# Six norms of the first block of a two-block transformer taken by token tiles, with their gains as rows

## What is computed

```python
def rmsnorm(x, g):
    xf = x.astype(jnp.float32)
    y = xf * lax.rsqrt(jnp.mean(xf * xf, axis=-1, keepdims=True) + EPS)
    return (y * g.astype(jnp.float32)).astype(x.dtype)

def first_block(x, ...):
    for l in range(DEPTH):
        x = x + 0.5 * swiglu(rmsnorm(x, g_ffn1[l]), w_ffn1_gu[l], w_ffn1_down[l])
        x = x + hybrid_mixer(rmsnorm(x, g_mix[l]), w_in[l], ...)
        x = x + 0.5 * swiglu(rmsnorm(x, g_ffn2[l]), w_ffn2_gu[l], w_ffn2_down[l])
    return rmsnorm(x, g_final)

def hybrid_layer(x, c, ...):            # second block, twice
    mod = jax.nn.silu(c) @ w_ada + b_ada
    sh1, sc1, gt1, sh2, sc2, gt2 = jnp.split(mod, 6, axis=-1)
    h = adaln(rms_norm(x, g_mix), sh1, sc1)
    ...
    x = x + gt1[:, None, :] * (mixed @ w_out)
    h = adaln(rms_norm(x, g_mlp), sh2, sc2)
    u = jnp.square(jax.nn.relu(h @ w_up))
    x = x + gt2[:, None, :] * (u @ w_down)
```

## Time and profile before

| what | us |
|---|---|
| median of 3 runs | 2094.83 |
| lowest, highest | 2093.02, 2095.72 |
| span of the profiled execution | 2091.6 |
| TensorE busy | 1985.8 (95%) |
| DVE busy | 1556.4 (74%) |
| ACT busy | 1017.8 (49%) |
| POOL busy | 37.0 (2%) |

### The profile page before, as it was taken

One profiled execution on the slowest core, in us unless ns is written; L12 is line 12 of the kernel. 1 busy time (PEld: TensorE's weight loads), 2 busy tenths in 40 slices (PEclk: granted clock), 3 DMA queues, 4 the chain that ended last, 5 costly groups with the idle time before them and its releaser, 6 DMA issues.

```text
span 2091.6 us, 32432 instructions
## 1 busy us (share of the span) xinstructions
PE 1985.8 (95%) x11828; PEld 1737.4 (83%) x11828; DVE 1556.4 (74%) x2748; ACT 1017.8 (49%) x1550; POOL 37.0 (2%) x72
## 2 busy tenths in 40 slices
PE   6999999989999999999899999998899979999998
PEld 5888988878888888898888887898688868887887
DVE  7887467679877887556688887775766768677766
ACT  5445444644445445445555445466444445554443
POOL 0000000000000000000000000000000000000000
PEclk9999999999999999999999998999999989998999
DMA  7774443247774775443246763431355534233553
GB/s 293 279 284 183 161 152 122 91 171 273 278 254 146 287 283 213 157 162 122 91 168 248 280 246 123 179 147 59 133 181 184 194 138 180 93 125 113 190 189 133
DMA packets 76900, 382.05 MB, mean 183 GB/s; under 512 B 8960, under 2 KB 9088, under 8 KB 55552
## 3 DMA queue, kind: packets, MB, share of 16 engines
q1 hardware_dynamic: 67392, 329.78, 43.0%
q0 software_dynamic: 9408, 50.90, 7.0%
HBM read 379.60 MB, written 1.05 MB: 182 GB/s over the span
## 4 chain that ended last, share of the span: by engine, by line
PE 83%; DVE 10%; ACT 4%; issue 2%; DMA 1%; SPq 0%; DVEq 0%; ACTq 0%
PE psum L641 20%; PE psum L557 16%; PE psum L559 15%; PE psum L558 15%; PE psum L644 10%; DVE weights_low_a L1366 2%; ACT weights_high_a L1029 1%; PE psum L875 1%; DVE weights_low_b L1366 1%; PE psum L605 1%; DVE h_high_low L1415 1%; PE psum L877 1%; PE psum L850 1%; PE psum L876 1%; PE psum L788 1%
## 5 line engine op out<-in xcount | busy, mean ns | idle before, releaser
L641 PE MATMUL psum<-h_high_low,weights_high_a 128*128 128x512 f32 x1840 | 665.8, 403 | 7.4 <-DVE h_high_low L1411 4.6
L1366 DVE TENSOR_TENSOR weights_low_a<-raw_a,weights_high_a 128x2048 fp32r<-128x2048 f32 (+1 forms) x232 | 460.0, 1984 | 124.4 <-ACT weights_high_a L1029 121.8
L644 PE MATMUL psum<-h_high_low,weights_low_a 128*128 128x256 f32 x1840 | 518.5, 282 | 0.0
L1029 ACT ACTIVATE weights_high_a<-raw_a 128x2048 fp32r<-128x2048 f32 (+1 forms) x232 | 386.1, 1664 | 126.6 <-PE psum L559 122.8
L641 PEld LDWEIGHTS psum<-h_high_low,weights_high_a 128*128 128x128 f32 x1840 | 349.8, 190 | 100.4 <-DVE h_high_low L1415 6.4
L644 PEld LDWEIGHTS psum<-h_high_low,weights_low_a 128*128 128x128 f32 x1840 | 351.5, 191 | 7.0 <-issue 1.0
L1366 DVE TENSOR_TENSOR weights_low_b<-raw_b,weights_high_b 128x1024 fp32r<-128x1024 f32 x224 | 273.4, 1221 | 55.9 <-ACT weights_high_b L1029 55.1
L1029 ACT ACTIVATE weights_high_b<-raw_b 128x1024 fp32r<-128x1024 f32 x224 | 236.0, 1054 | 109.5 <-PE psum L559 109.4
L1080 ACT ACTIVATE up_low_products<-psum 128x512 f32<-128x512 f32 (+1 forms) x146 | 74.0, 507 | 407.1 <-PE psum L644 407.1
L557 PE MATMUL psum<-weights_high_b,gated_high 128*128 128x512 f32 x608 | 240.4, 395 | 1.0 <-DVE gated_low L1484 1.0
L558 PE MATMUL psum<-weights_low_b,gated_high 128*128 128x512 f32 x608 | 240.5, 396 | 0.0
(11 more groups left out here) (296 smaller groups left out, 3226.6 us busy)
## 6 DMA issues: line engine op xcount, KB each, us to landing
ada_weights<-in_w_ada POOLq DMA_DIRECT2D x64, 768.0 KB, 5.7
raw_a<-in_w_ffn_a_a SPq DMA_DIRECT2D x44, 1024.0 KB, 7.2
raw_a<-in_w_ffn_b_a SPq DMA_DIRECT2D x44, 1024.0 KB, 7.2
raw_a<-in_w_ffn_a SPq DMA_DIRECT2D x64, 512.0 KB, 4.5
raw_b<-in_w_ffn_b SPq DMA_DIRECT2D x64, 512.0 KB, 3.2
raw_a<-in_w_proj_a SPq DMA_DIRECT2D x28, 1024.0 KB, 5.5
raw_a<-in_w_gate_a SPq DMA_DIRECT2D x26, 1024.0 KB, 4.8
raw_b<-in_w_ffn_a_b SPq DMA_DIRECT2D x44, 512.0 KB, 3.5
```

Of the source, the lines that this page charges most:

```text
L641: pe.matmul(ps[:, bank, :], whi[0][:, p, c:c + P], hboth[:, k, :, :].rearrange("p a b -> p (a b)"), start=k == 0, stop=False, skip_group_c ...
L644: last_mm = pe.matmul(ps[:, bank, SEQ:2 * SEQ], wlo[0][:, p, c:c + P], hhi[:, k, :], start=False, stop=k == KD - 1, skip_group_check=True)
L1029: act.activation(whi[kind][:, p, 0:width], raw[kind][:, p, 0:width], ACT.Copy).then_inc(now().hi_ready[kind], 1)
L1366: dve.tensor_tensor(wlo[kind][:, p, 0:width], raw[kind][:, p, 0:width], whi[kind][:, p, 0:width].bitcast(F32), ALU.subtract).then_inc(lo_r ...
```

## The change

1. **The six norms of the first block (`row_norm`).** The gain comes as a row of 128x1024, loaded by POOL's queue (`load_gain`, 512 KB each, two buffers in turn), instead of as a column. DVE multiplies x by the row factor and by the gain at once, in two halves of 128x512 for each tile (L1544). TensorE transposes tile 0 (8 transposes into banks 2 and 3), works on it, then transposes tile 1 (banks 4 and 5). ACT writes h high in two copies of 128x4x128 for each tile, DVE h low in two subtractions of the same size (L1551). DVE does the last sum of x, (1,1), after the scale of tile 0, and the scale of tile 1 after the low part of tile 0. The squares of the second tile's second half stand behind high(0) on ACT.
2. **First step after a norm by token tiles.** `first_gate_up` does the first gate-up step as pieces of 128 tokens: 64 multiplies instead of 32 (L689, 2x128 columns, and L691, 128 columns). In a projection (`project_rows`) tile 0's first piece comes before `second_tile()`. The ada columns are cut in 9 before the first transposes and 15 after the second ones.
3. **Ada bank.** The ada columns of the first block go to bank 1 and no longer wait for `x_ready`; only those ahead of norm 7 keep bank 4 and the wait.
4. **Last downs.** The last two `down` steps of every feed-forward run as (j-1: 00, 01, 10), (j: 00, 01), (j-1: 11), (j: 10, 11).
5. **Tail of w_out.** Rows 0 to 4 are done in all pieces, then rows 5, 6 and 7 per piece (`OUT_TAIL = 5`), in the mixers of both blocks. The splits of the next b0 are taken out of the merge and put after the norm.
6. **Next layer's a0, a1.** In a feed-forward that closes a layer, ACT splits the next layer's a0 and a1 in its last two steps, and DVE makes the low part of a0 before the last gate chain.
7. **Small.** Block 1's PSUM banks for projections follow a list of 8; the final gain comes in the same two buffers; parameters of the first block are narrower by 24 columns.

```diff
+OUT_TAIL = 5
...
-ROW_BANKS = 6
+ROW_BANK = {1: (0, 6, 7, 2, 3, 4, 5, 1), 2: (0, 1, 2, 3, 4, 5)}
...
                     retire_last_layer(k, blk)
                 if blk == 1:
 
-                    pool.wait_ge(now().scale_ready, 2 * NT + 1)
+                    pool.wait_ge(now().scale_ready, 2 * NT)
+                    load_gain(3 * l + 1)
+                    load_gain(3 * l + 2)
+                    pool.wait_ge(now().scale_ready, 4 * NT + 1)
+                    load_gain(3 * l + 3)
                     ada_loads(l, 1)
...
+                def turn(t):
+                    for half in range(2):
+                        pe.wait_ge(now().scale_ready, 2 * NT * (n - 1) + 2 * t + half + 1)
+                        for i in range(KD // 2):
+                            k = half * (KD // 2) + i
+                            m = pe.transpose(ps[:, ROW_TURN_BANK + 2 * t + half, i * P:(i + 1) * P],
+                                             xn[:, t, k * P:(k + 1) * P], ident)
+                        m.then_inc(now().turned, 1)
+
+                def second():
+                    turn(1)
+                    if ada:
+                        ada[0](ADA_FIRST, ADA_COLUMNS)
+
+                if ada:
+                    ada[0](0, ADA_FIRST)
+                turn(0)
+                state["h_waited"] = 0
+                state["halves"] = True
+                state["second"] = second
+                state["ada_copied"] = ada[1] if ada else None
...
+                def first_gate_up():
+
+                    wait_ffn_part(l, blk, 0, n0, 0)
+                    early = 1 if state["ada_copied"] else gates
+
+                    def piece(m, t):
+                        for k in range(KD):
+                            need_h(k, t)
+                            c = (m * KD + k) * P
+                            out = ps[:, m, :].rearrange("p (a b) -> p a b", a=2)
+                            cols = slice(t * P, (t + 1) * P)
+                            pe.matmul(out[:, :, cols], whi[0][:, 0, c:c + P], hboth[:, k, :, cols],
+                                      start=k == 0, stop=False, skip_group_check=True)
+                            last_mm = pe.matmul(out[:, 1, cols], wlo[0][:, 0, c:c + P], hhi[:, k, cols],
+                                                start=False, stop=k == KD - 1, skip_group_check=True)
+                        return last_mm
+
+                    for m in range(early):
+                        piece(m, 0)
+                    second_tile()
+                    for m in range(early):
+                        last_mm = piece(m, 1)
+                    if early < gates:
+                        need_ada_bank()
+                        for t in range(NT):
+                            last_mm = piece(1, t)
+                    last_mm.then_inc(now().used[0], 1)
+
                 def gate_up(j, p):
-                    if isinstance(j, int) and j == 1:
-                        need_ada_bank()
+                    if isinstance(j, int) and j == 0 and state["halves"]:
+                        first_gate_up()
+                        return
                     wait_ffn_part(l, blk, 0, n0, j)
...
+                def last_downs():
+
+                    j, p = tiles - 1, (tiles - 1) % 2
+                    need_down(j - 1)
+                    for t, h in ((0, 0), (0, 1), (1, 0)):
+                        down_piece(1 - p, t, h, False, False)
+                    need_down(j)
+                    for h in range(2):
+                        down_piece(p, 0, h, False, True).then_inc(now().sums_ready, 1)
+                    down_piece(1 - p, 1, 1, False, False).then_inc(now().used[1], 1)
+                    down_piece(p, 1, 0, False, True).then_inc(now().sums_ready, 1)
+                    down_piece(p, 1, 1, False, True).then_inc(now().used[1], 1)
 
...
+                for t in range(NT):
+                    for h in range(2):
+                        for k in range(OUT_TAIL, KD):
+                            m = out_piece(k, t, h)
+                            if k == OUT_TAIL and (t, h) == (NT - 1, 1):
+                                m.then_inc(now().used[1], 1)
+                        if (t, h) != (NT - 1, 1):
+                            m.then_inc(now().sums_ready, 1)
+                m.then_inc(now().used[0], 1)
 
...
+                def high(t):
+                    for half in range(2):
+                        seen(now().turned, "turned")
+                        k = half * (KD // 2)
+                        act.activation(hhi[:, k:k + KD // 2, t * P:(t + 1) * P],
+                                       ps[:, ROW_TURN_BANK + 2 * t + half, :].rearrange("p (k c) -> p k c", c=P),
...
+                if first:
+                    split_high(0, 1, 0, 0)
+                high(0)
+                row_guess(1, first)
+                high(1)
+                if after:
+                    after()
+
...
+            def next_layer_high(n):
+
+                k = layer_at[0]
+                if k + 1 < 2 * LAYERS:
+                    enter_layer(k + 1)
+                    split_high((k + 1) % LAYERS, (k + 1) // LAYERS + 1, 0, n)
+                    enter_layer(k)
+
...
-                        split_high(l, blk, 1, n0 + j + 1)
+                        if not closing:
+                            split_high(l, blk, 1, n0 + j + 1)
+                        if n0 and j >= tiles - 2:
+                            next_layer_high(j + 2 - tiles)
...
+                def scale(t):
+                    row_factor(t)
+                    for half in range(2):
+                        c = slice(half * 512, (half + 1) * 512)
+                        dve.scalar_tensor_tensor(xn[:, t, c], x[:, t, c], rstd[:, t:t + 1], gain[:, c],
+                                                 ALU.mult, ALU.mult).then_inc(now().scale_ready, 1)
+
+                def low(t):
+                    for half in range(2):
+                        seen(now().hhi_ready, "hhi")
+                        k, cols = slice(half * (KD // 2), (half + 1) * (KD // 2)), slice(t * P, (t + 1) * P)
+                        dve.tensor_tensor(hlo[:, k, cols],
+                                          ps[:, ROW_TURN_BANK + 2 * t + half, :].rearrange("p (k c) -> p k c", c=P),
+                                          hhi[:, k, cols].bitcast(F32), ALU.subtract).then_inc(now().hlo_ready, 1)
+
+                if update:
+                    update(0, 0)
+                    update(0, 1)
+                    update(1, 0)
+                scale(0)
+                if update:
+                    update(1, 1)
+                if between:
+                    between()
+                low(0)
+                scale(1)
+                low(1)
+                if after:
+                    after()
...
+                        await_next_layer(dve, n0)
+                        next_layer_low(0)
...
-                        merge(l, 1, Walk(SLOTS1, FF1 + 16, 3, YT1, G_AT[1]), FF1 + 16, 3, False)
-                        norm(lambda k: g(16 + k), after=lambda: split_low(l, 1, 0, FF1 + 23))
-                        feed_forward(l, 1, FF1 + 22, FF1, 2)
+                        update = merge(l, 1, Walk(SLOTS1, FF1 + 16, 3, YT1, G_AT[1]), FF1 + 16, 3, False)
+                        row_norm(3 * l + 2, update=update,
+                                 after=lambda: (split_low(l, 1, 0, FF1 + 23), split_low(l, 1, 1, FF1 + 22)))
+                        pending_update = feed_forward(l, 1, FF1 + 22, FF1, 2)
```

338 lines of the change are left out of this document (195 added, 143 removed).

## The result

The changed kernel takes 2099.66 us in the median of 20 runs, the kernel before 2094.78 in 20 runs beside it: a ratio of 1.0026, with an interval of 1.0018 to 1.0035, so some 5 us slower. The forecast was +6.55 against the profiled span. The profiled execution of after has a span of 2099.3, 7.7 above that of before. Stretches at half clock don't fall on the same places in every execution.

What follows compares the result with a forecast made beforehand. TensorE, busy 95% of the span, was taken as the bound. Terms of 3.9 + 0.8 + 0.8 + 4.0 + 2.0 + 1.4 - 6.35 gave +6.55 on 2091.6, 2098.2, and 2101.3 as median; range 2089 to 2107.

Steps and rivals of the forecast that it cites:

- my 3.2 between span and median: Whole kernel: the median of the runs lies 3.2 us above the profiled span, added to 2098.2 to give 2101.3.
- The gain's load: Norm 1: 512 KB of gain rows on POOL's queue make the slots land later by 0 to 1.3 us, taken 0.6.
- The second turn: Norm 1: DVE scales tile 1 after low(0), so TensorE waits about 1.1 us at tile 1's transposes.
- The small multiplies: Norm 1: the first gate-up step by token tiles costs 2.2 us more, partly at half clock.
- the 2.05: Norms 3 and 6: tile 1's scale, turn, copy and low part hold TensorE for 2.05 us.
- B: Rival, first steps: full clock and 128-column multiplies priced by their columns, -10.2 us in all, 2084.6; chance 0.13.
- The two stretches of half clock per norm: Norms 2, 4, 5: two stretches without wide multiplies, 3.4 us of half clock each in norm 4, 2.9 in 2 and 5.
- rival A: Norms 2 to 6: the clock stays full in the broken stretches, -3.2 us against the forecast, 2091.6; chance 0.26.
- the stall for the second slot: Norm 7: the second slot's low part, now first after the norm, takes 1.2 us off the 2.26 stall.
- first sum earlier by the tail: Norms 8 and 10: the first sum comes earlier and DVE runs through four sums with the scale, -0.85 us each.
- C: Rival, first steps: the 128-column multiply (L691) costs 0.15 us, +4.9 in all, 2106.2; chance 0.08.
- D: Rival: the first turn is late because ACT's and DVE's row_norm wait for each other, +0.6 us in five norms, 2104; chance 0.07.

Runs made afterwards that it cites:

- e1: The changed kernel with the first block's six norms as they were before, all else of the change kept: 2088.21 us, ratio 0.9971.
- e4: The kernel before, with the final gain's 512 KB load moved to POOL's queue at the start: 2098.77 us in one run.
- e10: The changed kernel with the last two down steps in their old order, four pieces each: 2104.88 us in one run.
- e3: The changed kernel with ada multiplies of 128 columns instead of 2: 2090.39 us, ratio 0.9984.
- e9: The kernel before, with the tile of ones 128 columns wide but ada multiplies still using 2, so later tiles move in SBUF: 2088.63 us, ratio 0.9973.
- e6: The changed kernel with the first block's old norms and ada multiplies of 128 columns (edits of e1 and e3 together): 2081.54 us, ratio 0.9934.
- e11: As e8, but with only the last two rows of w_out piece by piece instead of three: 2070.17 us, ratio 0.9889.
- e2: The changed kernel with tile 1 turned directly behind tile 0, all ada columns first and whole tokens in the first gate-up step: 2121.91 us, ratio 1.0133.
- e5: The kernel before, with ada multiplies of 128 columns instead of 2: 2081.67 us, ratio 0.9942.
- e8: As e6, with a0's low part where DVE waits and the new last-downs order only where a feed-forward closes a layer: 2070.75 us, ratio 0.9886.
- e7: The changed kernel with DVE's low part of the next layer's a0 back behind the scales: 2110.60 us in one run.

## Why the prediction was right, and where not

1. **The sum.** +6.55 was forecast, and the profile has +7.7, the medians +5. In the 20 runs of the changed kernel a time is 1.6 to 2.1 above its span; so 1.4 of my 3.2 between span and median came from a profiled execution that was faster than the median. The cause was right too: the norms by tiles cost more than the rest of the change gives (e1). The places are not as good as the sum: norms 2, 4 and 5 are off by +2.6, -2.0 and -1.8 and norm 10 by -1.15, and these errors cancel in part. That is luck.
2. **Norm 1, 3.9 forecast, 5.4 measured, above my range of 3.0 to 4.8.** Three terms were mis-sized. The gain's load had 0.6 (0 to 1.3) and is 1.5 in the changed kernel and 1.7 in e4. The DMA share is 0.96 to 1.04 in every window of 3 us from 3 to 18 us of the traces before, after and e4, so there was no spare time. The second turn had 1.1 and is 2.0 (1.05 of transposes, 0.98 of wait for h). The small multiplies had 2.2 and cost 1.4.
3. **Norms 3 and 6, 0.8 each.** Right in sum and in parts: gap shorter by 2.8 (2.9), second turn 2.03 (2.05), pair 0.23 (0.23). The terms written for the 2.05 are 3.2 less 3.7, which doesn't give it; that the number came out is luck. B's price of 0.06 for a 128-column multiply was true, but its partner of 2x128 columns costs 0.17, not the 0.118 of 256 in one run; the two together cost what two 2-column multiplies do. So B's gain was not there.
4. **Norms 4, 2, 5: 7.4 forecast, 6.2 measured** in the profile (+1.4 in the mixers behind). The wait for gated_low is 1.20 in norm 4 (1.35) and 1.22 for 0.51 in norm 2 (+0.7), though e10 shows that in norm 5 taking it away gains nothing. The two stretches of half clock per norm came in norm 2, twice as long as I took them (6.8 for 3.4); in norms 4 and 5 the trace has one short fall each. e3 puts both halves of the forecast to the test, since its clock is full there: its norms 2, 4 and 5 stand at -1.2, +0.4 and -1.9, where the forecast without its clock terms has -0.9, +0.55 and -1.5, and its whole profile at -3.1, where rival A has -3.2. (Some 2.5 us of this are e3's faster feed-forwards, which e9 has too, so the match of the whole is in part chance.) What the clock costs is then the changed kernel less e3: 5.8, 1.6 and 1.5, where the forecast had 2.9, 3.45 and 2.9. The sum of these is right (8.9 for 9.25) and no single one is. Rival A is thus wrong at norm 2 and half right at 4 and 5. That a fall may hit or miss is in the 10 us of spread of both kernels.
5. **Block 2, -6.35 forecast, -6.8 measured.** The sum is right and owes much to where the clock fell. Norm 9 (-2.6 for -2.5) and the end (-0.8 for -0.7) hold in the other traces too. Norm 7 has -1.6 (-1.45), but 0 in e1, e3 and e6. Its parts: h comes 0.3 earlier behind the longer wait for gated_low, as forecast (1.5 less 1.25); the stall for the second slot was to fall by 1.2 and fell by 0.2, and what stands in for it is that the first slot's products take 1.05 less, with 1.4 us of half clock under them instead of 3.4. Norms 8 and 10 have -1.75 together (-1.7), as +0.2 and -2.0: the first wait is 0.8 shorter as forecast (2.95 for 3.78), but at equal half clock norm 10 gains 0.1 to 0.7 only. The reason given (first sum earlier by the tail) falls with e11.
6. **Rivals.** C is refuted by the 0.23 of a pair, D by the 3.1 of the gap in norm 3. D's mechanism is there all the same, in the second tile, where ACT's and DVE's order leaves 2.0 to TensorE (and the 3.5 of e2).
7. **Not seen.** That a term of this size comes with where tiles lie in SBUF (e9), and that half clock, which the kernel before also has, could be had out of it for nothing (e5). And that the change takes half clock away elsewhere: from 26 us on, the trace after has 96 us of it, the trace before 116, though norm 2 has 6.8 more.

## What to carry to other kernels

If work is taken by tiles on one engine, look at the queues of the others: tile 1's chain ran behind all of tile 0's on ACT and DVE, which cost 2.0 in norm 3, and with the 1.8 of the smaller multiplies that is more than the 2.8 of the shorter first wait. Split work that nobody waits for yet belongs where its engine already waits (e8), neither in front of a gate chain nor in front of the first h. Where TensorE has many short multiplies, their clock shows in the windows: making them wider cost nothing here and gave some 6 us. And before a small gain is credited to a reordering, look where the half clock lies in both traces: in norms 7, 8 and 10 it decided more than the order did.

## What the runs showed of the hardware

- A multiply of 2 columns and one of 128 columns take the same 0.11 us behind weights of the same size (e5), but only with the narrow ones did the granted clock fall to 0.50 in norms 2, 4 and 5; with the wide ones it stayed at 1.00 there (e3, e5, e6).
- In pairs on 2x128 and 128 columns, the spacing is 0.17 and 0.06 rather than twice 0.115.
- 504 bytes of shift in SBUF changed the spacing of 512-column multiplies by up to 0.006 us (0.233 to 0.227) and the median by 0.27% (e9). Which operand's address does it wasn't tried.
- The clock's falls aren't the same in every execution: norms 1 to 3 are the same code in the changed kernel and in e7 and differ by 0.05 us at most, while another order of the last downs ahead of norm 2 (e10) made it 2.9 shorter, 0.7 of it the wait for gated_low.
- A fall of the clock costs half its length where TensorE has work: the 16 wide pairs of a first step took 8.4 us instead of 5.6 with the clock at 0.50 for 5.9 of them (e2, norm 3).
